# ScalarE instead of VectorE reads the product banks of the stage `even_in`

## The reference, cut to what matters

```
def even_mixer(x, w_in, b_in, ml_norm, w_out):
    u = x @ w_in + b_in
    mq, mk, mv, mo, mi, mf, fq, fk, fv, ff = split_sizes(u, [HALF, HALF, HALF, HALF, ML_HEADS, ML_HEADS, HALF, HALF, HALF, FOX_HEADS])
    ...
```

## Time and profile before

| | |
|---|---|
| median of three runs | 2297.35 us (2295.97 to 2300.35) |
| the profiled execution | 2297.78 us, its span 2296.0 us |
| mean granted clock of TensorE | 0.961 |
| busy, share of the span | TensorE 95%, VectorE 44%, ScalarE 36%, GpSimd 36% |
| chain that ended last | TensorE 87%, VectorE 9%, ScalarE 2% |

### The profile page before, as it was taken

One profiled execution on the slowest core, in us unless ns is written; L12 is line 12 of the kernel. 1 busy time (PEld: TensorE's weight loads), 2 busy tenths in 40 slices (PEclk: granted clock), 3 DMA queues, 4 the chain that ended last, 5 costly groups with the idle time before them and its releaser, 6 DMA issues.

```text
span 2296.0 us, 29683 instructions
## 1 busy us (share of the span) xinstructions
PE 2182.6 (95%) x12396; PEld 1754.9 (76%) x12404; DVE 1008.6 (44%) x1636; ACT 830.9 (36%) x1268; POOL 818.6 (36%) x362
## 2 busy tenths in 40 slices
PE   8999989999899999999997899999999889999997
PEld 6767788888778888776776688888877477888886
DVE  4222855436531121345337644442268465444323
ACT  4345511134342242232335344442243334444322
POOL 4423300034244444442231344444444024444442
PEclk9999988799999999999999899999999989999998
DMA  7222200014223233221111122232312012322331
GB/s 264 92 69 83 74 2 3 2 56 156 74 83 101 92 101 101 83 73 65 47 56 40 53 92 92 96 104 95 101 57 90 19 55 65 102 100 92 101 98 58
DMA packets 53005, 182.97 MB, mean 80 GB/s; under 512 B 5752, under 2 KB 5760, under 8 KB 52744
## 3 DMA queue, kind: packets, MB, share of 16 engines
q1 hardware_dynamic: 52872, 181.08, 23.6%
HBM read 176.32 MB, written 7.62 MB: 80 GB/s over the span
## 4 chain that ended last, share of the span: by engine, by line
PE 87%; DVE 9%; ACT 2%; issue 1%; POOL 1%; DMA 0%; DVEq 0%; SPq 0%; ACTq 0%
PE ps L321 19%; PE ps L323 19%; PE ps L322 19%; PE ps L1506 3%; PE ps L2500 2%; PE ps L341 1%; PE ps L2502 1%; PE ps L347 1%; PE ps L2501 1%; PE ps L342 1%; PE ps L1036 1%; PE ps L3036 1%; PE ps L434 1%; PE ps L1038 1%; PE ps L1037 1%
## 5 line engine op out<-in xcount | busy, mean ns | idle before, releaser
L178 POOL TENSOR_TENSOR split_units<-raw_units,split_units 128x1024 fp32r<-128x1024 f32 x314 | 760.2, 2429 | 1423.2 <-ACT split_units L169 1423.2
L321 PE MATMUL ps<-x_split,split_units 128*128 128x512 f32 x1224 | 482.8, 394 | 8.6 <-POOL split_units L178 6.3
L169 ACT ACTIVATE split_units<-raw_units 128x1024 fp32r<-128x1024 f32 x314 | 329.9, 1052 | 437.9 <-PE ps L323 380.1
L322 PE MATMUL ps<-x_split,split_units 128*128 128x512 f32 x1224 | 478.2, 391 | 0.0
L323 PE MATMUL ps<-x_split,split_units 128*128 128x512 f32 x1224 | 477.9, 390 | 0.0
L321 PEld LDWEIGHTS ps<-x_split,split_units 128*128 128x128 f32 x1224 | 230.9, 189 | 62.8 <-issue 6.5
L322 PEld LDWEIGHTS ps<-x_split,split_units 128*128 128x128 f32 x1224 | 230.9, 189 | 49.2 <-issue 1.7
L323 PEld LDWEIGHTS ps<-x_split,split_units 128*128 128x128 f32 x1224 | 230.9, 189 | 48.6
L321 PE MATMUL ps<-hidden_split,split_units 128*128 128x512 f32 x608 | 237.3, 390 | 0.0
L323 PE MATMUL ps<-hidden_split,split_units 128*128 128x512 f32 x608 | 236.6, 389 | 0.0
L322 PE MATMUL ps<-hidden_split,split_units 128*128 128x512 f32 x608 | 236.5, 389 | 0.0
(11 more groups left out here) (434 smaller groups left out, 3283.9 us busy)
## 6 DMA issues: line engine op xcount, KB each, us to landing
raw_units<-stream SPq DMA_DIRECT2D x314, 512.0 KB, 3.4
bias_rows<-bias_line SPq DMA_DIRECT2D x1, 2816.0 KB
gate_rows<-work SPq DMA_DIRECT2D x10, 256.0 KB, 2.1
work<-gate_rows SPq DMA_DIRECT2D x10, 256.0 KB, 2.7
x<-x_t SPq DMA_DIRECT2D x4, 512.0 KB, 6.5
work<-bias_rows SPq DMA_DIRECT2D x1, 2048.0 KB
out_t<-x SPq DMA_DIRECT2D x8, 256.0 KB
vec<-vectors SPq DMA_DIRECT2D x1, 1159.5 KB, 9.2
```

The source lines that it names most:

```text
L169: scalar.activation(self.split[:, u % SPLIT, 0, :], self.raw[:, u % RING, :], ACT.Copy).then_inc(self.high_done, 1)
L178: gpsimd.tensor_tensor(self.split[:, u % SPLIT, 1, :], self.raw[:, u % RING, :], self.split[:, u % SPLIT, 0, :].bitcast(F32), ALU.subtract ...
L321: TE.matmul(out, high, rhs(0, k), start=(k == 0), stop=False)
L322: TE.matmul(out, high, rhs(1, k), start=False, stop=False)
```

## The change

In `even_in` all 16 banks are read by ScalarE, in the loop in which it rounds the weights and after the rounding and the gates' work of the same n: tiles with Identity and a bias, the tiles of the queries (16 to 19) with the scale as well, turns with Copy. Since ScalarE computes `scale * x + bias`, where VectorE computed `(x + bias) * scale`, VectorE writes a scaled bias for those four tiles once, ahead of the gates' copy at n = 2. TensorE waits on `read_act` instead of `tile_read`. VectorE keeps only `gates_dve`, and goes from one part of it to the next without waiting for products. The second forget set (n = 9) and the last gate copy (n = 14) now signal `ready_out`; `pair_scores(0)` and the first scores of the mLSTM wait on it. `split_rows` got a parameter for that.

```diff
-        def split_rows(dve, rows, n, tile, j, rest, rounded):
+        def split_rows(dve, rows, n, tile, j, rest, rounded, done=None):
...
                 ins = V.tensor_copy(row_parts(tile, j)[32 * k:32 * k + n], part)
+                if k == 2 and done is not None:
+                    ins.then_inc(done.sem, 1)
+                    continue
...
+            scaled_bias = col[:, 32:36]
...
                     dve.wait_ge(side_pe.sem, side_pe.at(1))
+                    V.tensor_scalar(scaled_bias, v("ev_b", 16, 4), EVEN_SCALE[4], None, ALU.mult)
                     V.tensor_copy(w[0:16, GATES, :], ps[0:16, 4, :]).then_inc(side_dve.sem, 1)
...
-                    split_rows(dve, w[0:n, first, :], n, tile, j, ROWS + 6, ROWS + 7)
+                    split_rows(dve, w[0:n, first, :], n, tile, j, ROWS + 6, ROWS + 7, ready_out if m == 9 else None)
+                    if m == 9:
+                        dve.wait_ge(ready_out.sem, ready_out.at(1))
                 elif m == 14:
                     dve.wait_ge(side_pe.sem, side_pe.at(3))
-                    dve_chain.link(dve, V.tensor_copy(col[:, 16:32], bank(7, 0, 16)))
+                    V.tensor_copy(col[:, 16:32], bank(7, 0, 16)).then_inc(ready_out.sem, 1)
+                    dve.wait_ge(ready_out.sem, ready_out.at(2))
...
                     if n >= 4:
-                        pe.wait_ge(tile_read.sem, tile_read.at(n - 3))
+                        pe.wait_ge(read_act.sem, read_act.at(n - 3))
...
                 before.dve(dve)
-                for n, (kind, m) in enumerate(EVEN_FIRST):
-                    dve.wait_ge(tile_ready.sem, tile_ready.at(n + 1))
-                    if kind == "tile":
-                        even_tile(m, n % 4).then_inc(tile_read.sem, 1)
-                    else:
-                        V.tensor_copy(w[:, 40 + m, :], bank(n % 4)).then_inc(tile_read.sem, 1)
+                for n in range(n_jobs):
                     gates_dve(dve, n)
...
-                for n, (kind, _) in enumerate(EVEN_FIRST):
+                for n, (kind, m) in enumerate(EVEN_FIRST):
                     wts.round_high(act, S, u0 + tiles + SPLIT)
                     gates_act(act, n)
+                    act.wait_ge(tile_ready.sem, tile_ready.at(n + 1))
+                    if kind == "turn":
+                        ins = S.activation(w[:, 40 + m, :], bank(n % 4), ACT.Copy)
+                    elif m // 4 == 4:
+                        act.wait_ge(side_dve.sem, side_dve.at(1))
+                        ins = S.activation(w[:, m, :], bank(n % 4), ACT.Identity, scale=EVEN_SCALE[4],
+                                           bias=scaled_bias[:, m - 16:m - 15])
+                    else:
+                        ins = S.activation(w[:, m, :], bank(n % 4), ACT.Identity, bias=v("ev_b", m))
+                    ins.then_inc(read_act.sem, 1)
                     tiles += kind == "tile"
...
                     if p == 0:
-                        pe.wait_ge(tile_read.sem, tile_read.at(0))
+                        pe.wait_ge(read_act.sem, read_act.at(0))
+                        pe.wait_ge(ready_out.sem, ready_out.at(-1))
...
                         pe.wait_ge(tile_read.sem, tile_read.at(KEYS_DONE))
+                        pe.wait_ge(ready_out.sem, ready_out.at(0))
```

More of the change, by code:

```diff
@@ L2311, in stage_even_in @@
             tile_ready.close(n_jobs)
-            tile_read.close(n_jobs)
+            read_act.close(n_jobs)
+            ready_out.close(2)
             side_pe.close(3)
@@ L2489, in dense @@
                         if k == 0:
-                            pe.wait_ge(tile_read.sem, tile_read.at(b - 3 if b < 2 else b - 1))
+                            if b < 2:
+                                pe.wait_ge(read_act.sem, read_act.at(b - 3))
+                            else:
+                                pe.wait_ge(tile_read.sem, tile_read.at(b - 1))
                         if b == GATES_DONE and k == 0:
```

## The result

The changed kernel takes 2293.53 us (median of 21 runs, 2290.06 to 2299.61), the kernel before beside it 2299.54 (21 runs, 2293.92 to 2303.95). The ratio is 0.9977, with a 95% interval of 0.9970 to 0.9985. On the 2297.35 us of the forecast that is 5.3 us faster, between 3.4 and 6.9; the two medians are 6.0 apart. I had forecast 7.6 us, which lies outside that interval. The direction was right, and the time lies in the stated range, but the size was off by 2.3 us on this ratio. The profiled execution took 2295.65 us, of which 2293.9 are span: only 2.1 us less than the one of before.

What follows compares the result with a forecast made beforehand. TensorE bounds the kernel, pausing in `even_in` for VectorE's late bank read. From 2297.35 us, minus 7.6 (5.55 of pause, 2.1 of slow clock), came 2289.7 us; range for 8 in 10, 2286.3 to 2293.8.

Steps and rivals of the forecast that it cites:

- the place and the cause: In `even_in`, TensorE waits 5.6 us for VectorE's late read of turn 0, behind the gates' row work.
- the sum of the stage: In `even_in`, gain 7.6 us: 5.55 of pause, 2.1 from four transposes and seven matmuls at 1.2 GHz.
- the queue's own times: In `even_in`: first Exp 1012.5, last Ln done 1019.1, turns read by 1028.6, last tile 1051.1, first peak 1053.1.
- 11.0: New work on ScalarE in `even_in`: four turn reads at 0.60 and twelve tile reads at 0.72 us.
- the eight transposes: Turns 2 and 3 on TensorE: 0.79 us without a stall, from 1032.93 until 1033.72.
- VectorE's 31.3 us: VectorE's row work left without bank reads, begun at 1019.2; said to hold four pieces blocked by GpSimd already.
- The end of its rows: VectorE ends its row work in `even_in` near 1050.5 and idles 2 us before the first peak.
- the weighing of the page: ScalarE's table loads: the page's 1380 ns drain would give 2292.5 us; the trace shows 1.28 us and no drain.
- From `pair_scores(0)` to the end it stays 1236 us, give or take 2: After `even_in`, the rest of the program takes as long as before, so the stage's gain stays whole.
- rival C: Pauses after 1200 us: earlier arrival changes clock recoveries, lengthened by 1.6 us each outweighing 7.6; about 2299 us, chance 0.03.
- random signs should cancel: Over some ten pauses left after 1200 us, changes in the slow stretches should cancel to +-2 us.
- granted clock 1.00: On TensorE in the changed profile, the full clock is granted from 1030 to 1060 us.

Runs made afterwards that it cites:

- fill in the tail: 37 unused matmuls ahead of the transposes of mLSTM items 6, 9, 10 and 14: changed kernel 2289.71 and 2291.29 us, kernel before 2298.66 us.
- turns-only kernel: Kernel before, with ScalarE reading only the four turns and VectorE keeping all twelve tiles: 2300.92 us, ratio 1.0004.
- the filled pause: Kernel before, with 24 unused 128x512 matmuls ahead of turn 3, where TensorE waits: 2303.63 us, ratio 1.0012.
- the spread products: Changed kernel, with half of the gates' product between the steps of job 3 and the small products between those of job 4: 2297.43 us, ratio 0.9987.
- eight matmuls later: Changed kernel, with 8 unused 128x512 matmuls at the end of `even_in` on TensorE: 2296.09 us, ratio 0.9983.
- test by a shift of the arrival: Changed kernel, with 4 or 8 unused matmuls at the end of `even_in` on TensorE: 2291.70 us (0.9968) and 2296.09 us (0.9983).

## Why the prediction was right and where it was wrong

*Right:* the place and the cause. One wait of TensorE, for a bank behind VectorE's row work. Put back alone, it takes the gain away (0.9997).

*Right:* the sum of the stage. The forecast was 7.6 us; from the L460 reciprocal to the first peak it is 96.5 against 89.2 and 88.9, so 7.3 and 7.6. The first profile has a shorter slow stretch at the stage's start and the dip at 1003, which nearly cancel. Of the queue's own times (first Exp, last Ln, both turns, last tile, end of VectorE's rows, first peak) none was off by more than 0.5 us. Two sizes were a little off: 8.7 us on ScalarE instead of 11.0, and the eight transposes 0.85 us instead of 0.79. A reading was off as well: VectorE's 31.3 us hold six operations that GpSimd made long, not four (2.40 to 3.30 us each in the kernel before). The end of its rows came out right because the changed kernel has six too, at other rows, and that was luck.

*Right:* the weighing of the page. The block of four table loads ran from 1010.88 to 1018.81, each load followed by its operation within 0.02 us. The drain that the Trainium skill ("ScalarE: Activation LUTs", "What ACT_TABLE_LOAD costs") adds does not show in this trace either.

*Wrong:* the step "From `pair_scores(0)` to the end it stays 1236 us, give or take 2", and behind it rival C's "random signs should cancel". In the first changed profile that distance was 1241.7 us (`pair_scores(0)` issues at 1052.16), 5.6 more than before, all of it in matmuls at 1.2 GHz. From the first peak on, the six profiles of kernels with no pause in `even_in` and no fill in the tail read 1240.9, 1236.0, 1241.2, 1241.4, 1239.2 and 1238.4. The four with a pause of 4.4 to 5.6 us at the old place or a little ahead of it read 1235.3, 1235.2, 1235.8 and 1235.5. The turns-only kernel, whose pause of 5.4 us stands two jobs later, reads 1237.8. So without the pause a part of the executions loses up to 6 us after 1200 us. In the first set of timed runs 2.3 us of the 7.6 are missing. I had this as rival C, at 0.03 and in the form "slower than before", and priced its mean at zero in the forecast itself, which was the error: I should have carried a loss of 0 to 6 us as a term of the sum. The point "granted clock 1.00" held from 1030 to 1060, as stated; the stretch at 1003, without any pause, lies outside it and was in no term of the sum.

*What stays open.* The slow stretch at 175 us behind the first peak is in five profiles: the first changed one, the filled pause, the spread products, eight matmuls later, and turns only. The one at 195 us is in the first four of these. In the six other profiles without a fill in the tail the clock stays whole at both places, though the pause of 2.1 us ahead of the first is there in all. What decides it is not shown. The slow recovery in `even_in` is a likely part: of the six profiles without it five read 3 us or more above the four with it. But turns only has both a pause with its recovery and one of the stretches, and the two groups also differ in when they reach the tail (first peak at 1050.7 to 1058.9 us against 1060.7 to 1063.3), which no run separates from the recovery. The test by a shift of the arrival did not settle it, and each row of the table has one profiled execution, so the shares of good and bad executions are not known. The six profiles lose 4.1 us on average against the four, more than the 2.3 us of the timed runs.

## What to carry to other kernels

The gain of a pause taken from the engine that bounds the kernel is the pause and its slow recovery, and here that could be summed from one trace to some tenths of a microsecond (7.6 against 7.3 and 7.6). What the program does with the new arrival, at pauses that remain, is a term of its own, and it need not average to nothing: look for the later waits of the same engine and carry their slow stretches, at their worst, into the range. And where an in-order engine serves both a long side job and the banks, all its bank reads may have to move: here moving only the turns moved the pause two jobs on, whole (5.4 us). And compare windows of two kernels at the same work, not at the same time.

## What the runs showed of the hardware

TensorE's clock fell to 1.2 GHz without a pause, at 1003.1 us, behind the gates' 16-column products, one full tile and three small products (0.51 in the window above, TensorE busy all of it), in 5 of 13 profiles. That they are narrow is the likely reason and is not shown; with these products spread among full ones it did not fall in the one profile taken, and the spreading cost 1.6 us. Second, the same pause of 2.13 us left the clock whole in one execution (1.00) and was followed by half speed in another (0.66 over 5 us): the length of a pause alone does not tell what it costs. Third, filling a pause of 5.5 us with 24 matmuls whose result is thrown away took the slow recovery away and made the kernel 0.12% slower.
